# One layer pair of a hybrid decoder on one core: value projections interleaved with the first ten attention items, head scaling on ScalarE, sampled convolution products on VectorE

## What is computed

```python
proj = h @ w_in                      # (544, 1024) @ (1024, 2568)
a_in, q, k, v, fg = split(proj)      # 1024 | 512 | 512 | 512 | 8
q = rms_norm(q per head of 64, q_g); k = rms_norm(k per head of 64, k_g)
glu = val * sigmoid(gate)            # the two halves of a_in
out = causal depthwise conv of width 31 over glu (history in front) + conv_b
a_out = silu(layer_norm(out))
s = q k^T / 8 + f_q - f_k, causal    # 8 heads, f is the cumulated log forget gate
att = softmax(s) v                   # prompt: 4 query blocks of 128
x = x + concat(a_out, att) @ w_out   # the sampled tokens also attend to two cached pages each
```

## Time and profile before

| what | value |
|---|---|
| median of 3 runs | 1293.3 us |
| the profiled execution's own time | 1298.79 us |
| its span in the profile | 1297.0 us |
| PE busy | 1253.4 us (97%) |
| VectorE busy | 631.6 us (49%) |
| ScalarE busy | 450.6 us (35%) |
| GpSimd busy | 117.1 us (9%) |

### The profile page before, as it was taken

One profiled execution on the slowest core, in us unless ns is written; L12 is line 12 of the kernel. 1 busy time (PEld: TensorE's weight loads), 2 busy tenths in 40 slices (PEclk: granted clock), 3 DMA queues, 4 the chain that ended last, 5 costly groups with the idle time before them and its releaser, 6 DMA issues.

```text
span 1297.0 us, 23075 instructions
## 1 busy us (share of the span) xinstructions
PE 1253.4 (97%) x9778; PEld 1209.9 (93%) x9778; DVE 631.6 (49%) x910; ACT 450.6 (35%) x705; POOL 117.1 (9%) x136
## 2 busy tenths in 40 slices
PE   6988999889999999999999999989999999999998
PEld 5988995568999999999999999989999999999998
DVE  5599998644453343343343435653532433433431
ACT  5623436444332132132133334633321321322321
POOL 3042300001300000000001232042000000000000
PEclk9999997799999999999999999999999999999999
DMA  5321231152323223222323122212222322222312
GB/s 154 101 79 46 79 127 55 36 189 66 98 98 98 69 95 98 81 81 97 95 68 98 66 98 98 66 40 96 99 69 94 98 82 82 97 93 69 98 66 69
DMA packets 111755, 113.15 MB, mean 87 GB/s; under 512 B 6430, under 2 KB 105898, under 8 KB 111663
## 3 DMA queue, kind: packets, MB, share of 16 engines
q1 hardware_dynamic: 110111, 107.50, 25.9%
q0 software_dynamic: 1472, 4.41, 1.2%
q10 hardware_dynamic: 88, 0.02, 0.0%
HBM read 107.18 MB, written 5.16 MB: 87 GB/s over the span
## 4 chain that ended last, share of the span: by engine, by line
PE 83%; DVE 12%; ACT 2%; DMA 1%; POOL 1%; issue 1%; SPq 0%; ACTq 0%; DVEq 0%
PE ps L665 76%; DVE c_f L1536 5%; DVE w_lo L1459 1%; PE ps L815 1%; DMA w_raw<-in_w_in_ab 1%; PE ps L853 1%; PE ps L865 1%; PE ps L882 1%; DVE nat_buf L1610 1%; POOL A_lo L640 1%; DVE a_f L1870 1%; DVE n_small L1595 0%; PE ps L840 0%; DVE prob L1647 0%; PE ps L942 0%
## 5 line engine op out<-in xcount | busy, mean ns | idle before, releaser
L665 PE MATMUL ps<-A_hi,w_hi 128*128 128x272 f32 x1408 | 293.8, 290 | 8.2 <-DVE xT L1485 4.1
L665 PE MATMUL ps<-A_lo,w_hi 128*128 128x272 f32 x1408 | 291.9, 289 | 0.0
L665 PE MATMUL ps<-A_hi,w_lo 128*128 128x272 f32 x1408 | 291.3, 288 | 0.0
L1126 ACT ACTIVATE w_hi<-w_raw 128x1024 fp32r<-128x1024 f32 x180 | 189.0, 1051 | 265.6 <-DVE xT L1767 249.3
L665 PE MATMUL ps<-B_hi,w_hi 128*128 128x272 f32 x1280 | 265.9, 289 | 0.0
L665 PE MATMUL ps<-B_lo,w_hi 128*128 128x272 f32 x1280 | 264.9, 288 | 0.0
L665 PE MATMUL ps<-B_hi,w_lo 128*128 128x272 f32 x1280 | 264.0, 288 | 0.0
L665 PEld LDWEIGHTS ps<-A_hi,w_hi 128*128 128x128 f32 x1408 | 221.9, 189 | 9.8 <-ACT xT L1156 4.5
L665 PEld LDWEIGHTS ps<-A_hi,w_lo 128*128 128x128 f32 x1408 | 222.3, 189 | 0.0
L1459 DVE TENSOR_TENSOR w_lo<-w_raw,w_hi 128x1024 fp32r<-128x1024 f32 x180 | 219.7, 1221 | 4.3 <-ACT w_hi L1126 4.3
L665 PEld LDWEIGHTS ps<-A_lo,w_hi 128*128 128x128 f32 x1408 | 220.7, 189 | 0.0
(11 more groups left out here) (272 smaller groups left out, 1026.9 us busy)
## 6 DMA issues: line engine op xcount, KB each, us to landing
w_raw<-in_w_ff_up SPq DMA_DIRECT2D x64, 512.0 KB, 4.4
w_raw<-in_w_ff_down SPq DMA_DIRECT2D x64, 512.0 KB, 3.9
w_raw<-in_w_in_ab SPq DMA_DIRECT2D x20, 512.0 KB, 4.9
w_raw<-in_w_in_c SPq DMA_DIRECT2D x16, 512.0 KB, 4.2
w_raw<-in_w_out_ab SPq DMA_DIRECT2D x8, 512.0 KB, 4.6
k_pg<-in_cache_k SPq DMA_DIRECT2D x16, 256.0 KB, 4.4
v_pg<-in_cache_v SPq DMA_DIRECT2D x16, 256.0 KB, 3.1
w_raw<-in_w_out_c SPq DMA_DIRECT2D x8, 512.0 KB, 4.1
```

Source lines behind the costliest of these rows:

```text
L665: mm = pe.matmul(ps[:, 2 * s + half, 0:HALF], wt[:, j % 4, k, :], mv[:, k, half * HALF:(half + 1) * HALF], start=(k == 0 and at_ == 0), st ...
L1126: act.activation(w_hi[:, j % 4], w_raw[:, b % 2, :, P * (j % 2):P * (j % 2) + P], ACT.Copy)\
```

## The change

- The value projections m = 20..29 are mixed with attention: scores(0) and scores(1) stand behind m = 22, and `ITEMS` puts slots 0 to 9 behind m = 23..29. Slots 10 to 31 follow alone. Up to slot 10 the scores run two items ahead instead of three. Score banks are 2 and 3, later 6, 2 and 3; value projections use two banks (0, 1) instead of four; the transposed probabilities go to banks 4 and 5, the outputs to bank 7.
- `scale_heads` moves from VectorE to ScalarE, four activations of 64 columns each in place of one VectorE operation of 256. The factor needs no multiplication by `r_nat` any more, because the squares are taken unscaled and the root's bias is `e_nat` = 1e-6 / (r_nat squared). VectorE keeps the reciprocal (`head_factor`) and the key gain (`key_gain`, now two tiles behind).
- GpSimd's four products go; VectorE makes them into one buffer (`sampled_taps`), behind m = 3, 5, 12 and 15.
- The convolution starts behind tile j = 2 and takes 28, 25, 20 and 40 steps in the gated, query, key and value stages, and 11 behind slots 10 to 20. Block 0 runs ten taps alone, then two lanes run (blocks 0, 2 and blocks 1, 3).
- The three `split_lo` of the attention stage move to the sampled stage, behind b = 1, 2, 3. `forget_rows` moves from item 5 to slot 10, `sample_prep` from items 6..13 to 12..19, `LN_MEAN` from 22 to 25 and `LN_VAR` from 29 to 30. `channel_sums` use banks 0 and 1, so the sampled scores wait for the layer norm's root too.

```diff
-CONV_GLU, CONV_Q, CONV_K, CONV_V = [6, 6, 5, 2], (3, 3), (2, 2), 4
-CONV_ATT = [1] * 19 + [0] * 13
-SPLIT_ATT = (12, 15, 22)
-LN_MEAN, LN_VAR = 22, 29
+CONV_GLU = (0, 0, 4, 5, 6, 5, 6, 2)
+CONV_NAT = (3, 2, 4, 0, 4, 0, 3, 3, 2, 4,
+            3, 2, 0, 2, 3, 0, 2, 3, 2, 3,
+            4, 3, 3, 3, 5, 4, 5, 4, 5, 4)
+CONV_ATT = 1
+CONV_LEAD = 10
+SAMPLED_AT = {3: 0, 5: 1, 12: 2, 15: 3}
+ITEMS = {3: (0,), 4: (1, 2), 5: (3,), 6: (4, 5), 7: (6,), 8: (7, 8), 9: (9,)}
+FIRST_ALONE = 10
+LN_MEAN, LN_VAR = 25, 30
...
-                pool.tensor_tensor(prod[c % 2][:, :, :, :], window, taps, ALU.mult).then_inc(prod_done, 1)
...
+            def item_slot(s):
+                if s <= FIRST_ALONE:
+                    scores(s + 2)
+                elif s == FIRST_ALONE + 1:
+                    scores(s + 2)
+                    scores(s + 3)
+                elif s + 3 < n_items:
+                    scores(s + 3)
+                turn_probs(s)
+                if s % 2 == 0 and s >= 2:
+                    values(s // 2 - 1)
...
+                if m >= 4 * TT + 2:
+                    pe.wait_ge(v_evac, m - 4 * TT - 1)
...
-                if m == 6 * TT - 3:
+                if m == 4 * TT + 2:
                     scores(0)
+                    scores(1)
+                for s in ITEMS.get(m - 4 * TT, ()):
+                    item_slot(s)
...
+            def scale_heads(m):
+
+                n = NS if m % TT == 0 else P
+                act.wait_ge(head_ok, m + 1)
...
+                for h in range(4):
+                    a_ = act.activation(nat_buf[0:n, m % 3, h, 0:HD], nat_ps(m)[0:n, HD * h:HD * h + HD], ACT.Copy,
+                                        scale=n_small[0:n, 4 + m % 2, h:h + 1])
+                a_.then_inc(nat_evac, 1)
...
-                act.activation(n_small[0:n, 2 + m % 2, :], n_small[0:n, m % 2, :], ACT.Sqrt, bias=eps[0:n, 0:1],
+                act.activation(n_small[0:n, 2 + m % 2, :], n_small[0:n, m % 2, :], ACT.Sqrt, bias=e_nat[0:n, t:t + 1],
...
+            def sampled_taps(c):
+
+                taps = conv_wT[:, c, 0:TAPS].rearrange("p (a b w) -> p a b w", a=1, b=1).broadcast_to([P, NB, NQ, TAPS])
+                link(dve.tensor_tensor(prod[:, :, :, :], glu_window(c), taps, ALU.mult))
+                link(dve.tensor_reduce(c_f[:, c, 0:NS], prod[:, :, :, :].rearrange("p b q w -> p (b q) w"), AX_X, ALU.add))
...
-                link(dve.tensor_scalar(head, head, r_nat[0:n, t:t + 1], None, ALU.mult))
...
+                dve.reciprocal(n_small[0:n, 4 + m % 2, :], n_small[0:n, 2 + m % 2, :]).then_inc(head_ok, 1)
...
-                if s in SPLIT_ATT:
-                    n = N_OUT + SPLIT_ATT.index(s)
-                    split_lo(n, n)
...
+                if b in (1, 2, 3):
+                    n = N_OUT + b - 1
+                    split_lo(n, n)
```

More of the change, by code:

```diff
@@ L233, in build @@
                 for b in range(NB)]
-        prod = [at(f"prod{s}", [P, NB, NQ, TAPS], F32, spare + 4 * NS * TAPS * s) for s in range(2)]
+        prod = at("prod", [P, NB, NQ, TAPS], F32, spare)
         at_s = at("at_s", [P, PAIRS, NS], F32, zone_sq + 8 * KS)
@@ L821, in _ @@
[L821 to L844, removed]
-                if m == 6 * TT - 3:
-                    scores(0)
@@ L1618, in _ @@
[L1618 to L1632 removed]
+                if m >= 2:
+                    dve.wait_ge(nat_evac, m - 1)
@@ L1670, in centre, with item_slot @@
                 dve.wait_ge(cm_done, 1)
-                dve.scalar_tensor_tensor(out=two(c_f[:, c, :]), in0=ps[:, 6:8, 0:HALF], scalar=-1.0 / DA,
+                dve.scalar_tensor_tensor(out=two(c_f[:, c, :]), in0=ps[:, 0:2, 0:HALF], scalar=-1.0 / DA,
                                          in1=two(c_f[:, c, :]), op0=ALU.mult, op1=ALU.add).then_inc(cx_done, 1)
-            for s in range(H * QT):
-                if s == 0:
-                    for first in range(3):
-                        maximum(first)
-                    share(0)
-                    share(1)
-                if s + 3 < H * QT:
+            def item_slot(s):
+                if s <= FIRST_ALONE:
+                    maximum(s + 2)
+                    share(s + 1)
+                elif s == FIRST_ALONE + 1:
+                    maximum(s + 2)
@@ new lines, in _ @@
+            for m in range(6 * TT):
+                if 2 * TT <= m - 2 < 4 * TT:
+                    key_gain(m - 2)
+                if m < 4 * TT:
+                    sums(m)
+                if 1 <= m < 4 * TT + 1:
+                    head_factor(m - 1)
+                if m == 1:
+                    split_lo(11, 11)
+                if m == 4 * TT + 2:
+                    maximum(0)
+                    maximum(1)
+                    share(0)
+                for s in ITEMS.get(m - 4 * TT, ()):
+                    item_slot(s)
+                if TT < m < 5 * TT and m % TT in (1, 3):
+                    n = N_NAT + 2 * (m // TT - 1) + m % TT // 2 + 4
+                    split_lo(n, n)
+                if m in SAMPLED_AT:
+                    sampled_taps(SAMPLED_AT[m])
+                conv(CONV_NAT[m])
@@ L1687, in _ @@
+            for s in range(FIRST_ALONE, H * QT):
+                item_slot(s)
+                if s == FIRST_ALONE:
                     forget_rows()
-                conv(CONV_ATT[s])
-                if s in SPLIT_ATT:
-                    n = N_OUT + SPLIT_ATT.index(s)
-                    split_lo(n, n)
+                conv(CONV_ATT)
                 if s in (LN_MEAN + 2, LN_MEAN + 3):
```

235 lines of the change are left out of this document (136 added, 99 removed).

## The result

The changed kernel takes 1288.0 us (median of 6 runs, 1286.4 to 1292.4) and the kernel before, on the same chip, 1294.9 (6 runs): a ratio of 0.9945 [0.9928, 0.9962]. That is 6.9 us faster; 16.8 were forecast, and 1288.0 lies 1 us above the range. The profiled spans are 1297.0 and 1290.6; both profiled executions are longer than their kernel's median, the changed kernel's being the longest of its six (1292.4 us, with a granted clock of 0.988 against 0.991 or 0.992 in the others), so a stage in a profile can be longer than it mostly is. From the second turn of the sampled heads on (the transposition of `own` at 298.60 and at 292.38), the kernels take 998.4 and 998.2 us, so the difference lies in the mixer's stages.

The account below looks back on a forecast made before the run. The prediction took PE to bound gated tiles, keys and values, and VectorE the queries. Gains of 8.9, 7.5 and 3.1 us, less 2.2 and 0.5, made 16.8 off 1293.3: 1276.5 us, range 1267 to 1287.

Parts of the forecast that it names:

- Queries: Gated and query stages: VectorE leaves the gated tiles at about 88 us instead of 95.3; PE's 1.60 and 2.56 waits go.
- The first rival: Queries and keys: ScalarE's chain bounds them, 20 rounds take 77 us, the first gain falls to nothing, time 1285; 14%.
- the step that took VectorE's slack as cover: Queries and keys: VectorE's 61 us hide behind PE's 68, some 6 us of slack; m = 20 starts 8.9 us earlier.
- Mixed stage: Ten value products with slots 0 to 9: 44.5 us instead of 52.0, 7.5 us gained.
- the third rival: Mixed stage: the clock falls to 1.2 GHz because products wait for late VectorE shares; 24 us more, time 1300; 8%.
- Slots 10 to 31: Attention items after the mixed stage: 49 us instead of 52.1 with one stretch at 1.2 GHz kept, 3.1 us gained.
- The idle time before scores(14): Near slot 11: PE idles about 3 us while scores(14) waits for `forget_rows`, then a stretch at 1.2 GHz.
- The second rival: Slots 10 to 31: the stretch at 1.2 GHz, costing about 6 us, doesn't come, so time 1270; 14%.
- Sampled stage: Sampled attention: splits ahead of the copy of page b = 3 delay it; 2.2 us lost, between 0 and 3.4.
- start of m = 20: End of queries and keys: the first value product starts near 153.0 us instead of 161.9, 8.9 us gained.
- the 0.5 kept for small waits: No particular place: 0.5 us taken off the summed gain of 17.3 for small waits that couldn't be placed.
- fourth rival: Mixed stage: PE waits as long as it did in attention and the first rival holds too; 1291 to 1295; 4%.

Follow-up runs that it names:

- Run 9: Changed kernel with the sampled-tap products back on GpSimd, their sums behind gated tiles 5, 6, 7 and in round 2: 1298.5 us, ratio 1.0030 to the kernel before.
- run 7: Changed kernel with the head scaling back on VectorE, one product of 256 columns per block: 1289.9 us, ratio 0.9952 to the kernel before.
- run 4: Changed kernel with the key gain behind a round's first convolution step instead of a round later: 1289.4 us, ratio 0.9948 to the kernel before.
- Run 10: Changed kernel with all ten items (slots 0 to 9) behind the last value product, m = 29: 1295.3 us, ratio 0.9996 to the kernel before.
- run 2: Changed kernel with the four convolution steps behind m = 29 moved to slots 21 to 24: 1288.0 us, ratio 0.9935 to the kernel before.
- run 5: Changed kernel with the edits of run 1, run 2 and run 4 together: 1280.2 us, ratio 0.9885 to the kernel before.
- run 11: kernel 6 with ScalarE's last two weight splits moved from ahead of exponent(11) to slots 20 and 21: 1278.7 us, ratio 0.9865 to the kernel before.
- run 3: Changed kernel with 24 transpositions of the identity added in PE's wait before scores(14), results unused: 1295.8 us, ratio 0.9998 to the kernel before.
- Kernel 12: The kernel of run 11 with nine unused transpositions of the identity in PE's short waits around scores(12) to scores(14): 1278.6 us, ratio 0.9878 to the kernel before.
- run 1: Changed kernel with all three sampled-stage weight splits behind page b = 3: 1282.7 us, ratio 0.9891 to the kernel before.
- run 8: Changed kernel with the sampled-tap products back on GpSimd, their sums in rounds 1, 2, 4 and 6: 1304.2 us, ratio 1.0069 to the kernel before.
- kernel 6: The kernel of run 5 with GpSimd's stores of v behind the last exponent, no longer ahead of its memset: 1280.5 us, ratio 0.9885 to the kernel before.

## Why the prediction was wrong

The direction and two of the five stages were right; the size was not. The stage times are those of the two profiles.

**Queries: right.** VectorE was through with the gated tiles at 88.0 us (88 forecast; the two steps that start at 86.61 are the last), the waits of 1.60 and 2.56 went, and the stage became 8.4 us shorter. Run 9 puts the queries' whole gain on the four products and their sums in the gated stage, as the working from the earlier trace rows did. A product of 992 elements on VectorE took 1.15 us (1.1 taken), a 64-column scaling 0.316 (0.31 taken). The first rival did not come: in the queries the only wait of over 0.5 us for ScalarE is one of 0.58, and the scalings are worth 1.3 us on ScalarE (run 7).

**Keys: the step that took VectorE's slack as cover failed.** The sum said that VectorE had 6 us of slack over 20 rounds (68 less 61 is 7) and so cost nothing. In the trace it does have slack, 29.6 us busy in 35.9, and PE still waits, because a round's order counts and not its sum: the gain for block m - 2 stands behind everything VectorE does in round m - 1, and the heads can't be turned without it. 2.6 us were lost against the kernel before. Moving the gain gave 1.2 back (run 4); what is left stands behind the sampled products, which the same sum counted, 10.4 us, without asking what waits behind them.

**Mixed stage: right,** 44.7 against 44.5 us, with the clock at 1.00, the wait for the last copy of heads at 1.04 (1.0 forecast), and no sign of the third rival. Run 10 shows its worth.

**Slots 10 to 31: the term was mis-sized, -2.0 instead of +3.1 us.** It doesn't follow from its own working: 2.4 us of splits taken off VectorE, against 1.3 for two steps and 0.95 for `forget_rows` put on, leave next to nothing, and the 3 us of idle time come on top as a loss. The idle time before scores(14) came as forecast (2.90 against 3), and so did the stretch at 1.2 GHz. Missing was the wait of 1.26 us just ahead: VectorE's share took 1.99 us beside GpSimd's stores and memset. The other mistake was to count VectorE's lost splits as a gain while putting its four steps ahead of maximum(12). Without the four steps the stage is 50.4 us in run 2 and 51.6 in run 5, and with ScalarE's splits out of the way too it is 49.1 (run 11), the 49 that were forecast. The second rival never came: every profile has a stretch at 1.2 GHz in these slots. Its price of 6 us isn't settled, since the fillers of runs 3 and 12 didn't take the stretch away.

**Sampled stage: 5.8 us lost where 2.2 were taken.** The delay of page 3 was right: its copy starts 8.4 us into the stage (262.31), and 6.1 us into it with the splits behind it (run 1). What I left out is that PE's two waits bring the clock down, and that the sampled scores then run at half of it, 3.64 us instead of 1.93. I had reckoned with it at scores(14) and not here. The upper end of this term, 3.4, had no room for it. Run 1 shows the whole 5.8. How much of the 3.5 us comes differs between the profiles, and no run shows why: in run 8, with the same two waits, the first sampled scores ran at full clock and the stage lost 2.3 us, the term as forecast.

The shortfall, in us: start of m = 20, 2.1; mixed stage 0.2; slots 5.1; sampled stage 3.6; less the 0.5 kept for small waits. That is 10.5, against 10.4 between the forecast gain of 16.8 and the spans' 6.4; between the medians it is 9.9. My fourth rival said that gains would be given back, at 4%, but placed it in the mixed stage.

## What to carry to other kernels

Cost a moved block of work by what stands behind it in its new place, not by the slack of its engine: three splits and four convolution steps, 6 us of work, stand in the two stages that took back half of the 15.7 us that two others won, and putting them and the key gain elsewhere made the kernel 0.6% faster again (run 5). Give every wait of PE that you forecast a second price, for the matmuls behind it at half the clock, as a range: the same two waits cost 2.3 to 5.8 us here. Before you fill a wait to hold the clock, look for the next wait, because the fall may only move there (runs 3 and 12). The same goes for moving a wait away: three stood at the same place here (the four steps, stores and memset, ScalarE's splits), and removing the second after the first won nothing.

## What the runs showed of the hardware

A VectorE operation with one input from SBUF, the share of 256 columns, takes 0.35 us, and 1.99 us when it starts while GpSimd issues its stores and has the memset next: at 200.41 in the changed kernel, with GpSimd's rows at the same time. It ended at 202.40, as the memset did at 202.25.

```profile
200.41 1.99 DVE L1688 TENSOR_SCALAR prob<-prob,soft 128x256 f32<-128x256 f32 x1
```

```profile
200.01 0.75 POOL L497 DMA_DIRECT2D out_v_prompt<-v_nat  x1 [38.53 <-ACT v_nat L1237]
200.76 0.53 POOL L497 DMA_DIRECT2D out_v_sample<-v_nat  x1
201.28 0.97 POOL L607 MEMSET q_bd<- 128x1024 f32 x1
```

Which of the two did it isn't settled; in kernel 6 a share beside the stores, with no memset behind, took its normal 0.49 us for 512 columns. With the products, whole steps were held for 1.6 to 2.1 us each (run 9). The Trainium skill, SBUF — State Buffer (Who interferes with whom), says that VectorE and GpSimd share a pair of ports as an exclusive lock, for VectorE's operations with two SBUF inputs against a GpSimd operation that reads SBUF, and for its two-port modes against any. The trace agrees on the steps and splits beside the products (6.96 us for four against 2.7). Whether the share ran in a two-port mode no trace here shows.

The other surprise is run 3: 24 extra matmuls from 202.2 us on, and 6 us lost far behind them. Kernel 12, with nine such matmuls, didn't show it.
